# Modulation products in six units of four feature groups instead of twenty-four single groups

## The reference

```
mod   = silu(c)     @ w_ada[l] + b_ada[l]      # 1024 x 6144, six vectors of 1024
mod_c = silu(c_ctx) @ w_ada[l] + b_ada[l]
h = layernorm(x) * (1 + scale1) + shift1 -> mixer -> x = layernorm(ALPHA*x + gate1*y)
h = layernorm(x) * (1 + scale2) + shift2 -> ffn   -> x = layernorm(ALPHA*x + gate2*y)
```

## Time and profile before

| what | value |
|---|---|
| three runs | 3038.22, 3041.12, 3042.14 us, median 3041.12 |
| span of the profiled execution | 3040.4 us |
| median of the runs less that span | 0.7 us |
| PE busy | 2869.7 us, 94% of the span |
| DVE, ACT, POOL busy | 43%, 44%, 45% |
| HBM read | 355.51 MB, 117 GB/s over the span |
| granted TensorE clock, mean | 0.976 of full speed |

### The profile page before, as it was taken

How to read it: one execution, slowest core, us unless ns; L and a number is a source line. 1 busy time by engine, 2 the same in 40 slices (tenths; PEclk the granted TensorE clock), 3 DMA queues, 4 the chain that set the end, 5 groups by cost and what they waited for, 6 DMA issues and landing times.

```text
span 3040.4 us, 45574 instructions
## 1 busy us (share of the span) xinstructions
PE 2869.7 (94%) x19100; PEld 2462.3 (81%) x19100; DVE 1300.0 (43%) x2725; ACT 1323.9 (44%) x2220; POOL 1380.3 (45%) x646
## 2 busy tenths in 40 slices
PE   7999998899999999998999899899998999999998
PEld 5778876688876888877788698899986799877898
DVE  3777767532234111015677653332236341164440
ACT  3254433323424322225454346444554564544563
POOL 3432030244432543435422176578652488532686
PEclk9999999999999999999999999999999999998999
DMA  6332022133324343334211154445443255431454
GB/s 238 117 104 81 28 77 81 45 118 97 118 79 168 118 145 125 116 117 172 91 54 42 42 160 147 125 157 181 151 134 108 91 182 173 130 130 51 133 181 123
DMA packets 103555, 359.50 MB, mean 118 GB/s; under 512 B 11126, under 2 KB 17526, under 8 KB 102840
## 3 DMA queue, kind: packets, MB, share of 16 engines
q1 hardware_dynamic: 103352, 356.60, 36.1%
HBM read 355.51 MB, written 1.05 MB: 117 GB/s over the span
## 4 chain that ended last, share of the span: by engine, by line
PE 83%; DVE 7%; ACT 5%; POOL 3%; issue 1%; DMA 1%; SPq 0%; ACTq 0%; DVEq 0%
PE PS L357 83%; POOL RINGL L2496 2%; ACT AR L1147 1%; DVE AR L1779 1%; ACT WH L1127 1%; PE PS L368 1%; ACT XT L1147 1%; DVE SM L2013 1%; ACT L1147 1%; DVE XT L1779 1%; DVE AR L1783 0%; POOL HTR L2501 0%; DVE AR L1787 0%; DVE AR L1940 0%; DVE AR L2032 0%
## 5 line engine op out<-in xcount | busy, mean ns | idle before, releaser
L2496 POOL TENSOR_TENSOR RINGL<-RING,WH 128x1024 fp32r<-128x1024 f32 (+1 forms) x554 | 1299.1, 2357 | 1549.0 <-ACT WH L1127 1548.3
L357 PE MATMUL PS<-HTR,WH 128*128 128x256 f32 (+2 forms) x2736 | 877.0, 322 | 0.0
L1127 ACT ACTIVATE WH<-RING 128x1024 fp32r<-128x1024 f32 (+1 forms) x554 | 568.6, 1035 | 653.9 <-PE PS L357 524.3
L357 PE MATMUL PS<-HTH,WH 128*128 128x256 f32 (+1 forms) x2336 | 749.4, 322 | 25.5 <-POOL RINGL L2496 21.4
L357 PE MATMUL PS<-HTH,RINGL 128*128 128x256 f32 (+1 forms) x2336 | 727.4, 317 | 4.1 <-POOL RINGL L2496 4.1
L357 PE MATMUL PS<-ARR,WH 128*128 128x256 f32 (+2 forms) x2688 | 693.4, 326 | 18.0 <-ACT WH L1127 5.8
L357 PEld LDWEIGHTS PS<-HTR,WH 128*128 128x128 f32 (+1 forms) x2736 | 524.9, 192 | 40.4 <-issue 2.6
L357 PEld LDWEIGHTS PS<-ARR,WH 128*128 128x128 f32 (+1 forms) x2688 | 468.5, 192 | 65.1 <-issue 15.7
L357 PEld LDWEIGHTS PS<-HTH,WH 128*128 128x128 f32 x2336 | 449.7, 193 | 67.4 <-issue 30.8
L357 PEld LDWEIGHTS PS<-HTH,RINGL 128*128 128x128 f32 x2336 | 445.0, 192 | 33.5 <-POOL RINGL L2496 5.3
L357 PE MATMUL PS<-ARR,RINGL 128*128 128x256 f32 (+1 forms) x1472 | 467.0, 327 | 1.5 <-POOL RINGL L2496 1.5
(11 more groups left out here) (195 smaller groups left out, 3407.8 us busy)
## 6 DMA issues: line engine op xcount, KB each, us to landing
RING<-w_ada_in SPq DMA_DIRECT2D x96, 512.0 KB, 3.6
RING<-w_up_in SPq DMA_DIRECT2D x88, 512.0 KB, 4.2
RING<-w_gates_in SPq DMA_DIRECT2D x48, 512.0 KB, 3.5
RING<-w_ff_gate_in SPq DMA_DIRECT2D x44, 512.0 KB, 4.2
RING<-w_ff_up_in SPq DMA_DIRECT2D x44, 512.0 KB, 3.7
RING<-w_glu_in SPq DMA_DIRECT2D x32, 512.0 KB, 4.3
RING<-w_ff_down_in SPq DMA_DIRECT2D x32, 512.0 KB, 3.5
RING<-w_in_in SPq DMA_DIRECT2D x32, 512.0 KB, 3.6
```

The costliest lines, as they stand in the source:

```text
L357: return e.matmul(out_, lhsT, rhs, start=start, stop=stop)
L1127: e.activation(RINGS[name][:, j, 0:width], RING[:, b % NSLOT, 0:width], ACT.Copy).then_inc(*a_upper.up(b))
L2496: e.tensor_tensor(RINGL[:, i, 0:width], RING[:, i, 0:width], RINGS[name][:, j, 0:width], ALU.subtract).then_inc(*g_lower.up(b))
```

## The change

The twenty-four groups become six units `u = a // 4` of four groups, 2048 features each. The four strips of the array now hold four different groups, and the eight pieces of the contraction follow each other in the same PSUM bank, where they are summed. A block of `w_ada` is one piece by 1024 features. One row copy, four turning products with a matrix of eight columns (`PICK`) and one bias addition finish a unit. Calls of `fill` are where they were and still load four blocks each; the row copy of a unit falls to every fourth call (a % 4 == 0), the turning products and the bias to the call after it.

The second part of the change: the `fill_all` at the end of layer 0 goes from between ("p", 0, 2) and ("m", 1, 1) to the inside of ("m", 1, 1), on PE behind the spreading of rstd, on ACT behind the root, on DVE behind the modulation.

The hunks below are those of PE's `ada_rows`, `ada_turn`, `fill` and `fill_all`, of its `layernorm` and of its program for a layer, and then ACT's `fill` and `layernorm`.

```diff
             def ada_rows(a):
-                l, g = a // 12, a % 12
-                o = bank(6 + a % 2 if a < 4 or a >= 12 else 6, "ada", a, until=(a_ada, "row", a))
+                u = a // 4
+                if a % 4 == 0:
+                    bank(7 if u == 4 else 6, "ada", u, until=(a_ada, "row", u))
+                o = ps("ada", u)
                 pe.wait_ge(*a_ada.to("silu"))
-                for q in range(4):
-                    n, w, _ = load(A["w_ada"][l, 4 * g + q, :, :], 1024, False)
-                    for j in range(2):
-                        c = 64 * (q % 2) + 32 * j
-                        t = mm(o[c:c + 32, :], SCP[:, 2 * q + j, :], w[:, 512 * j:512 * j + 512], q < 2, q >= 2)
-                    t.then_inc(*p_block.up(n))
-                p_block.also("ada", a)
+                for k in (2 * (a % 4), 2 * (a % 4) + 1):
+                    for half in range(2):
+                        n, w, _ = load(A["w_ada"][u // 3, 16 * (u % 3) + 2 * k + half, :, :], 1024, False)
+                        for j in range(2):
+                            c = 64 * half + 32 * j
+                            t = mm(o[c:c + 32, :], SCP[:, k, :], w[:, 512 * j:512 * j + 512], k == 0, k == 7)
+                        t.then_inc(*p_block.up(n))
+                if a % 4 == 3:
+                    p_block.also("ada", u)
...
                 for j in range(4):
-                    t = mm(o[:, 2 * j:2 * j + 2], ROW[a % 2][:, 128 * j:128 * j + 128], FOLD2, True, True)
+                    t = mm(o[:, 8 * j:8 * j + 8], ROW[u % 2][:, 128 * j:128 * j + 128], PICK, True, True)
...
             def fill(n):
                 for _ in range(n):
                     a, lo, hi = ada_at
                     if a < hi:
-                        if a - 2 >= lo:
-                            ada_turn(a - 2)
+                        if a % 4 == 1 and a - 1 > lo:
+                            ada_turn(a // 4 - 1)
                         ada_rows(a)
                         ada_at[0] += 1
             def fill_all():
                 fill(100)
-                ada_turn(ada_at[2] - 2)
-                ada_turn(ada_at[2] - 1)
+                ada_turn(ada_at[2] // 4 - 1)
...
                 out_of_strips(o, RSTD, n).then_inc(*p_norm.up("rstd", *nid))
+                if nid == ("m", 1, 1):
+                    fill_all()
...
                 if not last:
-                    fill_all()
                     ring("WH0")
                     layernorm(("m", l + 1, 1), XT, lambda k: pe.wait_ge(*a_norm.to("post", l, 2, k)), BOTH)
...
             def fill(n):
                 for _ in range(n):
                     a, lo, hi = ada_at
                     if a < hi:
-                        if a - 1 >= lo:
-                            ada_row(a - 1)
+                        if a % 4 == 0 and a > lo:
+                            ada_row(a // 4 - 1)
                         ada_at[0] += 1
...
                 root(RSTD[:, 0:n // 4], ps("var", *nid)[:, 0:n // 4], done).then_inc(*a_norm.up("sd", *nid))
+                if nid == ("m", 1, 1):
+                    fill_all()
                 if then is not None:
                     then()
```

More of the change, by code:

```diff
@@ L140, in program @@
         ROPE = sb("ROPE", [P, 2, 256])
-        COL = sb("COL", [P, NCOL + 4])
+        COL = sb("COL", [P, NCOL + 10])
         MOD = sb("MOD", [P, 2, 48, 2])
@@ L195, in ps @@
             return banks[bank_of.get(label, 0)]
-        FOLD2 = COL[:, NCOL + 2:NCOL + 4]
+        PICK = COL[:, NCOL + 2:NCOL + 10]
         ROW = [ROWS[:, 0:512], ROWS[:, 512:1024]]
@@ L1147, in copy, with ada_row @@
                 return e.activation(out_, in_, f, bias=bias, scale=scale)
[L1149 to L1153, removed]
+            def ada_row(u):
+                act.wait_ge(*p_block.to("ada", u))
+                if u >= 2:
+                    act.wait_ge(*p_ada.to("turn", u - 2))
+                copy(ROW[u % 2], ps("ada", u)).then_inc(*a_ada.up("row", u))
             def fill(n):
@@ L1164, in fill_all @@
                 fill(100)
-                ada_row(ada_at[2] - 1)
+                ada_row(ada_at[2] // 4 - 1)
             def root(r, in_, done):
@@ L1196, in modulate @@
                     layernorm(nid, HT, cols, done, then)
-                act.wait_ge(*d_ada.to("one", 12 * l + 2 * scale + 1))
+                act.wait_ge(*d_ada.to("one", 3 * l + scale // 2))
                 p, c = norm_parts(nid, cols)[0]
@@ L1787, in stt, with ada_mod @@
                 return e.scalar_tensor_tensor(out=out_, in0=a, scalar=s, in1=b, op0=op0, op1=op1)
[L1789 to L1798, removed]
+            def ada_mod(u):
+                l, c = u // 3, 16 * (u % 3)
+                b = COL_AT["b_ada", l] + c
+                dve.wait_ge(*p_ada.to("turn", u))
+                tt(MOD[:, l, c:c + 16, :].rearrange("p (i j) n -> p i j n", i=4),
+                   ps("ada_turn", u)[:, 0:32].rearrange("p (j i n) -> p i j n", i=4, n=2),
+                   bc(COL[:, b:b + 16].rearrange("p (i j) -> p i j", i=4), 3, 2), ALU.add).then_inc(
+                       *d_ada.up("mod", u))
+                scales = {0: 8, 2: 32}.get(u % 3)
+                if scales is not None:
+                    m = MOD[:, l, scales:scales + 8, :]
+                    dve.wait_ge(*d_ada.to("mod", u))
+                    ts(m, m, 1.0, None, ALU.add).then_inc(*d_ada.up("one", u))
             def fill(n):
@@ L1803, in fill @@
                     if a < hi:
-                        if a - 2 >= lo:
-                            ada_mod(a - 2)
+                        if a % 4 == 1 and a - 1 > lo:
+                            ada_mod(a // 4 - 1)
                         ada_at[0] += 1
@@ L1842, in affine @@
                     if c.start == XA.start:
-                        dve.wait_ge(*d_ada.to("one", 12 * l + 2 * scale + 1))
+                        dve.wait_ge(*d_ada.to("one", 3 * l + scale // 2))
                         dve.wait_ge(*d_norm.to("mul", *part(nid, k, p)))
@@ L2281, in vector @@
                 if not last:
+                    modulate(("m", 1, 1), BOTH, 0, 1)
                     fill_all()
-                    modulate(("m", 1, 1), BOTH, 0, 1)
             def normed(nid, name):
@@ L2721, in arrange @@
     a["cc"] = np.concatenate([columns(inp["c"][0]), columns(inp["c_ctx"])], 1)
-    a["w_ada"] = by_tokens(inp["w_ada"], 512, 2)
+    a["w_ada"] = np.ascontiguousarray(inp["w_ada"].reshape(DEPTH, 8, 128, 3, 2, 1024).transpose(0, 3, 1, 4, 2, 5)
+                                      ).reshape(DEPTH, 48, 128, 1024)
     w = inp["w_in"]
```

16 lines of the change are left out of this document (7 added, 9 removed).

## The result

The changed kernel takes 3050.93 us (median of five runs, 3048.11 to 3054.99), the kernel before 3039.12 us in five runs beside it (3038.22 to 3042.14). The ratio is 1.0034, 95% interval [1.0024, 1.0045]: 11.8 us slower by the medians where 8.5 faster was forecast, outside the range of 3026 to 3040. The span is 3049.2 us against 3040.4, 8.8 longer (the profiled run before took 3041.12 us, 2.0 above its median), the mean granted clock 0.972 against 0.976, PE's busy time 2861.4 us against 2869.7. PE does less and ends later.

A forecast was written before the change was run, and what follows sets the result against it. PE bounds the kernel, holding 83% of the chain of waits and busy 94% of the span. Gains 1.0 + 6.4 + 5.7 + 4.2 = 17.3, losses 8.8, net 8.5: 3041.1 to 3032.6, forecast 3033, range 3026 to 3040.

The forecast's parts named there:

- deferral: Layer 1's w_glu: rounding of its first three blocks slips behind the modulated tiles, PE's first product 8.4 us later.
- start: Groups 0 to 3: without group 0's turning products the last transfers and layer 0's first product come 1.0 us earlier.
- first mixer: Groups 4 to 11: four waits for row copies go (2.74 us) and four groups' turning products (3.68), 6.4 gained.
- layernorms, FFN: Layer 0, groups 12 to 22: fewer row copies and turning products, 5.7 us gained, 3.3 of it in the feed-forward.
- passage: Layer 0 to layer 1: nothing between the layernorms, so the means follow ACT's scalings directly; 4.2 us gained.
- rival A: Passage to layer 1: the rounding is not deferred, or something hides it; 3024 us, chance 0.12.
- Rival C: Passage: late rounding, half clock and a second round trip through ACT cost more than all gains; 3046 us, chance 0.08.
- Half clock behind idle PE: After the passage: idle PE is followed by products at 1.2 GHz; 0.3 us lost, up to 5 kept for the range.
- Rival B: Mixer and feed-forward fills: blocks behind them are ready no earlier, so gains come back as waits; 3038 us, chance 0.20.
- The price of eight columns: Turning products with 8 columns where they had 2: 0 to 0.24 us more a unit, 0.1 taken in all.

The follow-up runs named there:

- e1: The changed kernel with the PSUM bank counter raised by 18 at the start of the second block, restoring the rotation; 3038.07 us, ratio 0.999.
- e3: The changed kernel with ACT rounding the first three blocks of layer 1's w_glu where it did before, ahead of the modulated tiles; 3045.78 us, ratio 1.0011.
- e5: The changed kernel with the hum of the second block's layernorm (1, 1) offset two banks further in the rotation; 3049.39 us, ratio 1.0029.
- e7: The changed kernel without the twelve hum products in front of and between the sums of layernorm (1, 1); 3043.67 us, ratio 1.0.
- e9: The changed kernel with layernorm (1, 1)'s sums in bank 0 instead of 6 (counter +2, then +6 behind them); 3041.14 us, ratio 1.0.
- e11: e4 with one more place in the three-bank rotation in front of the last pieces of the second block's attentions; 3035.21 us, ratio 0.9981.
- e12: e11 with the bank counter raised by 23 at the end of each attention, making 24 in total; 3033.1 us, ratio 0.9975.
- e2: The kernel before with the bank counter raised by 6 at the start of the second block, shifting the rotation as the change does; 3057.3 us, ratio 1.0048.
- e6: The kernel before with the hum of the second block's layernorm (1, 1) offset two banks back in the rotation; 3040.25 us, ratio 0.9995.
- e10: The kernel before with layernorm (1, 1)'s sums taken from bank 6 (counter +6, then +2 behind them); 3042.12 us, ratio 1.0005.
- e4: The changed kernel with both the bank counter raised by 18 and the rounding in its old place; 3032.36 us, ratio 0.9969.
- e8: The changed kernel with the rotation restored for the attention of layer 0 alone (+18, then +6 in front of the next layernorm); 3048.24 us, ratio 1.0021.

## Why the prediction was wrong, step by step

Fourteen traces stand against each other here, ten with the change's modulations (e1, e3 to e5, e7 to e9, e11, e12 and the changed kernel) and four without (before, e2, e6, e10). Gains are the difference of their means, positive is faster; for the deferral it is the six traces that have it against e3, e4, e11 and e12, for the second block the changed kernel's trace alone.

```
step                          forecast   mean gain   single traces, against before
start, to the first product     +1.0       -0.3      +1.2 to -2.9
first mixer, to 954.9           +6.4       +2.5      -0.2 to +6.5
layernorms, FFN, to 1371.7      +5.7       +5.1      +4.0 to +4.9
passage, to 1396.3              +4.2       +4.4      +3.6 to +4.4
deferral, in w_glu, to 1649.6   -8.7       -6.3      -5.1 to -10.1
second block                     0        -13.4      (changed kernel's trace)
```

**What failed is the sum: it has no term for the second block.** The prediction's part on what stays looked at loads and products, and its terms end at the passage. That the change does not touch the second block holds for its lines, not for its banks: `ada_turn` also has a side effect on a counter that every later stage reads, and 18 of its calls are gone. e1 and e2 show it in both directions, 13 to 16 and 15 us. Without it the change gains 4.0 us (e1 against its kernel before) where 8.5 were forecast, as the terms of the start and the mixer were too large.

**The deferral was right in mechanism and place, and near in size.** The first product came at R + 12.15 (forecast 4.0 + 8.4 = 12.4). Of these 8.1 us a part came back behind it: POOL makes eight tiles while PE is at half clock, and PE's three waits for POOL's later lower parts, 0.40, 1.12 and 1.13 us before, are two of 1.82 and 0.52. In medians it is 5 to 8 us (the square above). In single traces the size depends on one stretch at half clock: before has 6.8 us of it at 1454, the changed kernel and e3 have none, and there it is 5.3 + 2.2 = 7.5. So rival A's ground, that something hides the rounding, is refuted. Rival C had the right sign for a wrong reason: no second round trip of 8.4 us appeared (POOL waits 0.72 and 1.23 us for ACT's next upper parts, from 1410), and its 22 us at this place were 5 to 8. The time came out slower for what no rival named.

**Half clock behind idle PE** was expected at 0.3 us with up to 5 kept. PE by stretches, 8.63 us of waiting and then the products:

```profile
1390.00:1395.00 5.00, 1.28 (x12) 0.91 0.00 0
1395.00:1400.00 5.00, 0.08 (x1) 0.50 0.00 0
1400.00:1405.00 5.00, 5.00 (x26) 0.57 0.01 3
1405.00:1410.00 5.00, 5.00 (x44) 1.00 0.03 4
```

It lasts 10.2 us, about 4.4 of them under products. That this hides under POOL's tiles was argued and fits the rows; no run isolates it.

**The passage** is the best term: 4.2 forecast, 4.2 in the trace. The products of group 23 ran at half clock (2.77 us at 1375.27, forecast 3.2), the turn has its cover behind rstd.

**Layernorms and feed-forward.** 5.7 forecast, 4.5 in the changed kernel's trace and 5.1 in the means. The five fills of the feed-forward took it from -2.8 to -5.4, 2.6 against the 3.3 of the forecast. Rival B has these gains come back as waits; they did not.

**The first mixer** is mis-sized: 2.5 in the means. All waits for rows went as listed. Yet the same waits elsewhere are followed by 3.4, 6.8 or 10.2 us at half clock, differently in each execution. At 476 the changed kernel has 10.2 where before has 3.4, at 893 6.8 where before has 3.4, and each 3.4 us under full PE costs 1.7. The traces of e4, e9 and e11 gained 6.2 to 6.5, that of e8 none. By these, 6.4 is about what the edit gives when the clock gives the same; no run holds the clock fixed to show it.

**The start** gains nothing. The working said the end of the transfers would follow the slots that come free. In the trace PE's wait only grew (2.78 us where a turn had stood), because the transfers set the pace and the turns had lain under them. The scatter of the ten traces, 4.1 us, is larger than the term.

**The price of eight columns** was right: 0.96 us for a turn at full clock against 0.92.

## What to carry to other kernels

When an edit removes calls of a helper, list the helper's side effects as well as its instructions: counters of banks, buffers or blocks that later stages share. Here 18 fewer steps of one counter cost more than all that the edit saved, in code that the diff doesn't show; a shift by a multiple of every modulus in use (24 here) keeps the later stages as they were. e9 and e10, with 8, did not.

A warm-up product (the hum) helps only if it runs during the wait. Put one where a wait can come in front of it, and it becomes work at half clock on the path; asking for the next real product's bank behind the hum would be the first thing to try (it wasn't tried here). The hum needs a free bank as well, as e11 shows.

To compare two kernels, difference the same instruction's start at ten places before reasoning about a cause: it separated 9.8 us of gain from 18.6 of net loss here, and put 13.4 of the loss into code that the change doesn't touch. Do it for an improvement too: e11's lead was there before its edit ran.

## What was not expected of the hardware

The length of half clock behind the same wait differs: 5.33 us of idle PE in front of the same products were followed by 20.5 us of half clock in the changed kernel and 6.8 in e10, and 13.7 us in one piece begin between 2352 and 2371 in six traces (the changed kernel, e2, e5, e7, e9, e12), where the kernel before, e4, e6, e8 and e10 have none. The kernels whose waits shift about scatter more from run to run: e9 took 3031.57 to 3051.97 us with unchanged code, the fastest run at a mean clock of 0.977, the slowest at 0.972, while the kernel before keeps to 3035.21 to 3045.43 in 29 runs beside it. The Trainium skill (TensorE: Matmul & The Clock Gate, What's actually happening) says that one kernel can show different numbers of slow products from run to run; these traces agree, and here it is worth several us. A term of 1 to 3 us can't be read from one trace; it takes the same rows of many.

DVE's addition of 1 took 1.29 us, from 42.85 to 44.14, beside an instruction of POOL that ran from 41.75 to 44.11. Before it took 2.02 us for half the columns and ended with POOL's as well. By the lock of the Trainium skill (SBUF — State Buffer, Who interferes with whom) both should end so, and both traces agree.
